# Two weight loads of a streamed MoE layer, cut so that the last 3 and 2 KB of each row travel in transfers of 69, 57 and 2 rows

## What is computed

```python
def expert_block(args):
    xb, e = args
    h = xb @ w_up[e] + b_up[e]
    h_glu = jnp.minimum(h[:, :D_FF], SWIGLU_LIMIT)
    h_lin = jnp.clip(h[:, D_FF:], -SWIGLU_LIMIT, SWIGLU_LIMIT)
    act = h_glu * jax.nn.sigmoid(SWIGLU_ALPHA * h_glu) * (h_lin + 1.0)
    return act @ w_down[e] + b_down[e]
```

## Time and profile before

| | us |
|---|---|
| median of 3 executions | 1082.04 |
| lowest and highest | 1081.49, 1084.55 |
| the profiled execution's own time | 1081.66 |
| its span, first to last instruction | 1079.8 |
| PE busy in the span | 1065.2 |

### The profile page before, as it was taken

One profiled execution on the slowest core, in us unless ns is written; L12 is line 12 of the kernel. 1 busy time (PEld: TensorE's weight loads), 2 busy tenths in 40 slices (PEclk: granted clock), 3 DMA queues, 4 the chain that ended last, 5 costly groups with the idle time before them and its releaser, 6 DMA issues.

```text
span 1079.8 us, 13215 instructions
## 1 busy us (share of the span) xinstructions
PE 1065.2 (99%) x5687; PEld 445.8 (41%) x5688; DVE 361.4 (33%) x572; ACT 152.8 (14%) x302; POOL 11.9 (1%) x28
## 2 busy tenths in 40 slices
PE   9999999999999999999999999999999999999997
PEld 7888664333333333333333333333333333333332
DVE  3376534233322233332222233323232232232234
ACT  2121144111111101111111110011111101101113
POOL 1000010000000000000000000000000000000002
PEclk9999999999999999999999999999999999999999
DMA  8875969999999999999999999999999999999995
GB/s 291 305 276 199 402 214 390 419 425 426 427 429 433 431 430 429 433 427 434 429 429 429 434 431 430 429 429 432 433 432 427 432 430 433 423 427 428 424 413 188
DMA packets 45515, 431.47 MB, mean 400 GB/s; under 512 B 4968, under 2 KB 20364, under 8 KB 25872
## 3 DMA queue, kind: packets, MB, share of 16 engines
q1 hardware_dynamic: 44848, 430.41, 95.3%
q10 hardware_dynamic: 608, 0.20, 0.1%
HBM read 427.00 MB, written 3.48 MB: 399 GB/s over the span
## 4 chain that ended last, share of the span: by engine, by line
PE 87%; DMA 11%; issue 0%; ACT 0%; DVE 0%; POOLq 0%; DVEq 0%; ACTq 0%; POOL 0%
PE bank L1035 39%; PE bank L1054 16%; DMA ring_all<-in_w_up 10%; PE bank L716 9%; PE bank L1102 6%; PE bank L1009 4%; PE bank L1046 2%; PE bank L826 2%; PE bank L1017 2%; PE bank L1027 1%; PE bank L1095 1%; PE bank L669 1%; PE bank L1114 1%; DMA ring_all<-in_w_in 1%; PE bank L834 1%; PE bank L1140 1%
## 5 line engine op out<-in xcount | busy, mean ns | idle before, releaser
L1035 PE MATMUL bank<-ring_all,work 128*64 128x512 f32 x2040 | 482.9, 600 | 4.9 <-DMA ring_all<-in_w_up 4.9
L1035 PEld LDWEIGHTS bank<-ring_all,work 128*64 128x64 f32 x2040 | 133.9, 136 | 253.4 <-issue 243.9
L1054 PE MATMUL bank<-ring_all,work 128*64 128x512 f32 x992 | 225.3, 596 | 0.0
L1887 DVE TENSOR_TENSOR h_tok<-h_tok,bank 128x1024 f32<-128x1024 f32 (+1 forms) x67 | 81.7, 1220 | 234.2 <-PE bank L1102 228.3
L1054 PEld LDWEIGHTS bank<-ring_all,work 128*64 128x64 f32 x992 | 68.4, 137 | 128.1 <-issue 128.0
L716 PE MATMUL bank<-work,ring_all 128*128 128x264 f32 x384 | 87.1, 387 | 0.5 <-DMA ring_all<-in_w_in 0.5
L716 PEld LDWEIGHTS bank<-work,ring_all 128*128 128x128 f32 x384 | 72.3, 190 | 13.1 <-DMA ring_all<-in_w_in 1.1
L1857 DVE TENSOR_TENSOR work<-bank,bias_up 128x1024 f32<-128x1024 f32 x32 | 39.2, 1224 | 113.9 <-PE bank L1046 113.9
L1102 PE MATMUL bank<-work 64*128 64x512 f32 (+1 forms) x268 | 75.1, 637 | 0.0
L1874 DVE TENSOR_TENSOR work<-work 128x512 f32<-128x512 f32 x32 | 22.2, 692 | 106.5 <-ACT work L1453 106.4
L1437 ACT ACTIVATE work<-bank 128x264 f32<-128x264 f32 x32 | 12.5, 391 | 313.1 <-PE bank L1027 313.1
(11 more groups left out here) (238 smaller groups left out, 550.6 us busy)
## 6 DMA issues: line engine op xcount, KB each, us to landing
ring_all<-in_w_up SPq DMA_DIRECT2D x40, 4096.0 KB, 33.5
ring_all<-in_w_down SPq DMA_DIRECT2D x20, 4096.0 KB, 34.5
ring_all<-in_w_up SPq DMA_DIRECT2D x33, 2048.0 KB, 15.2
ring_all<-in_w_down SPq DMA_DIRECT2D x15, 2048.0 KB, 18.4
ring_all<-in_w_up SPq DMA_DIRECT2D x29, 1024.0 KB, 10.4
ring_all<-in_w_down SPq DMA_DIRECT2D x18, 1024.0 KB, 11.9
ring_all<-in_w_in SPq DMA_DIRECT2D x13, 1024.0 KB, 5.0
ring_all<-in_w_out SPq DMA_DIRECT2D x4, 1024.0 KB, 11.6
```

What stands on the lines that cost most here:

```text
L1035: mm = pe.matmul(bank[half * CAP:(half + 1) * CAP, up_bank(n) + b, :].rearrange("q (k p) -> q p k", k=KT), x, src[half][:, b * 512:(b + 1) ...
L1054: mm = pe.matmul(bank[half * CAP:(half + 1) * CAP, Y, :], av[:, 2 * i + k, :], src[:, k * D + half * 512:k * D + (half + 1) * 512], start= ...
L1887: tt(rows, rows, bank[0:m, b:b + 2, :], ALU.add).then_inc(comb_added, 1)
```

## The change

Two pairs are treated apart: the one with chunks 2 and 3 of `w_up` of expert 16 (chunks 96 and 97 of the list) and the one with chunks 2 and 3 of expert 25 (chunks 150 and 151). Of their 32 KB rows only the first 29 KB and the first 30 KB are fetched by the transfer of 128 rows. The remaining 768 and 512 floats of each row (3 KB and 2 KB) come by three more transfers, of rows 0 to 68, 69 to 125, and 126 to 127, issued right behind it on the same queue. All four raise the same semaphore, and the count that PE waits for is raised by 3 x 16 to match. Nothing else changes.

```diff
+UNEVEN = {(16, 2): 768, (25, 2): 512}
+FEW_ENGINES = (slice(0, 69), slice(69, 126), slice(126, 128))
...
+        uneven = {place["u", e, j]: cols for (e, j), cols in UNEVEN.items()}
...
-            seen[s % RING] += 1
+            seen[s % RING] += 1 + (len(FEW_ENGINES) if s in uneven else 0)
             signal.append((s % RING, 16 * seen[s % RING]))
...
                     if s in pairs:
                         sp.wait_ge(mm_done, s - RING + 2)
-                        sp.dma_start(ring_all[:, s % RING:s % RING + 2, :].rearrange("p a n -> p (a n)"),
-                                     pair_src(stream[s])).then_inc(landed[s % RING], 16)
+                        pair = ring_all[:, s % RING:s % RING + 2, :].rearrange("p a n -> p (a n)")
+                        cut = 8 * FF - uneven.get(s, 0)
+                        sp.dma_start(pair[:, 0:cut], pair_src(stream[s])[:, 0:cut]).then_inc(landed[s % RING], 16)
+                        if s in uneven:
+                            for few in FEW_ENGINES:
+                                sp.dma_start(pair[few, cut:], pair_src(stream[s])[few, cut:]).then_inc(landed[s % RING], 16)
                         continue
```

## The result

| | before | after |
|---|---|---|
| median | 1081.51 us (6 runs) | 1089.27 us (6 runs) |
| lowest and highest | 1080.96, 1084.55 | 1087.64, 1091.40 |
| the profiled execution | 1081.66 | 1090.00 |
| its span | 1079.8 | 1088.1 |

The ratio is 1.0064, 95% interval 1.005 to 1.0078: slower by 5 to 8 us. The forecast was 1091.5.

What follows compares the result with a forecast made beforehand. The weight stream and PE were taken as limits side by side. Carriers +10.0 and +6.7 us, less a 6.5 us lead, gave 10.2, trimmed to +9.5: median 1091.5 us, range 1082 to 1096.5.

Steps and rivals of the forecast that it cites:

- the shared path: Main case at both changed pairs: engines writing into the same partitions share one path, slowing the new rows; +9.5 us, chance 0.58.
- Nothing is shared: Rival at the changed pairs: engines are the limit, not where they write; about +0.2 us, 1082.3, chance 0.20.
- spread over many engines: Rival: the new narrow transfers run on many engines, so nothing is uneven; 1082.2 us, chance 0.06.
- The engines that gain nothing: At the changed pairs, engines relieved of rows were to gain nothing, their own rows waiting beside the new ones.
- The carriers' rate: Three engines bringing the new rows (carriers) get 0.45 of full rate at both pairs: +16.7 us for a carrier.
- The two side figures of the sum: The total recomputed at other rates for the new rows: +8.2 us at 0.49, +12.3 us at 0.40.
- The lead: Earliest engines are 6.5 us ahead of the last at 916 us, bounds 5 to 8, absorbing that much lateness.
- the run-out: End of the stream: few engines late, most done early, shown by a share of 0.2 for 6 us or more.
- the carriers are not the early ones: Rival: engines bringing the new rows have no lead to spend; 1088.7 or 1098.7 us, chance 0.14.
- Where PE stands: PE's weight waits grow from 4.9 to about 14 us, first between 640 and 720 us, largest just behind 867.
- SP: Six more issues on SP, up to 0.45 us each, 2.7 us; covered by its waiting, so cost nothing.

Runs made afterwards that it cites:

- the two halves: Ten pairs' 3 KB tails (experts 9 to 18) by two transfers of 64 rows, against one of 128 rows: 1110.49 us, ratio 1.0271 to the kernel before.
- the two phases of three rows: Load-only kernel, three-row transfers of 16 KB behind whole pairs: 0.611 us a row into those engines' own partitions, 1.25 us into three others'.
- six carriers: Changed kernel with tails in transfers of 114, 12 and 2 rows, so six engines carry about half as much each: 1091.29 us, ratio 1.0086.
- the run with the second portion in two: Changed kernel with expert 25's 2 KB tails replaced by 1 KB each at experts 24 and 26: 1090.82 us, ratio 1.0077.

## Why the prediction was right

**Direction, mechanism and size.** +9.5 us was forecast and +7.8 measured between the medians, 5.4 to 8.4 by the ratio's interval; the shared path was the likeliest case, and it is what the runs show. The size owes something to luck, since two terms were wrong in opposite directions (below). "Nothing is shared" fell with the two halves (+28 us) and the two phases of three rows; "spread over many engines" with the share of 0.19.

**The engines that gain nothing.** This is the step that was wrong, though the sum hides it. The text said of the fourth engine that it "gains nothing, since its own rows wait beside it". It loses. The windows of the changed kernel move 330 instead of 436 GB/s from 595 to 610 and 379 instead of 432 from 860 to 880, which is 1.59 and 1.06 MB, at 431 GB/s 3.7 and 2.5 us of the whole stream, not of three engines. Its packet records say the same: 29 KB rows take 1.21 us on the mean where the single transfer of 128 rows has 1.11. Followed from row to row, an engine without new rows takes from 587.8 to 609.8 us for eight rows of 29 KB and eight of 32 KB, 22.0 us, which at 1.10 and 1.215 us a row are 18.5. The pair issued at 867.7 before and at 870.6 after is the same one. Its signals from the engines of the late group came in by 906.2 before and by 910.5 after, 4.2 us later, although each of them had 1.5 us fewer to do. It stays hidden in the sum, because in the changed kernel the carriers end behind them.

**The carriers' rate.** Taken as 0.45 of the full rate, measured 0.200 and 0.135 us a row against 0.121 and 0.085, that is 0.61 and 0.63. The term is 43 x 0.200 - 0.9 = 7.7 and 43 x 0.135 - 0.6 = 5.2, 12.9 us instead of 16.7. It was too large by 3.8. What was missing is that the carriers' own whole rows are slowed as well: in the pair behind each changed one they take 1.24 to 1.37 us instead of 1.215, which is 0.2 to 1.2 us for eight rows. The last signals of that pair come at 914.8 instead of 906.2, +8.6 us, in the profiled executions, whose times differ by 8.3. The two side figures of the sum don't come out of it: with the same 0.7 taken off, the working at a rate of 0.49 gives +8.0 and not +8.2, and a rate of 0.40 gives +11.8 and not +12.3.

**The lead.** 6.5 us was an estimate from the run-out. By the signals of that same pair before, seven engines were through within 2.6 us of the first, and the other nine between 5.0 and 6.7. After the change three come at 9.5, 10.5 and 11.4 us behind the first, four are left within 1.4, and a fifth comes at 3.2. A signal doesn't name its engine, but the packet records of the first changed pair, followed from row to row, show that the carriers were early ones: they began their 3 KB rows at 596.7, 598.1 and 598.1 us, while the last of the other engines was through with its 29 KB rows at 604.0. So "the carriers are not the early ones" fell. At the second pair they were early no longer (their part of it ended at 867.2, 868.4 and 869.8, that of the others between 861.7 and 868.8): the lead is spent once, as the sum had it. With six carriers, the three added ones had less lead.

Where the lead comes from was not asked in the prediction, and the packets suggest an answer. Between 150 and 1066 us the kernel before has 39 packets of 16 KB on a queue of the kind "instruction". An engine that takes one needs mostly 11.26 us for eight rows instead of 9.72. Those 39 times 1.5 us over nine engines are 6.5 us, about the distance of the late group. Most of those that could be followed fell on late engines. No run tried it.

**Where PE stands.** Forecast: waits of about 14 us, measured 11.3. The first was expected between 640 and 720 and ended at 626.9, a little early; the largest just behind 867, and it was 5.05 us, ending at 876.3. PE hardly noticed the first pair, as said, with no wait at 609; its last signal came at 607.6 instead of 603.4, 4.2 us later where 5 was forecast. The run-out was to show a share of 0.2 for 6 us or more. It shows 0.60, 0.18 and 0.06 in windows of 2 us from 1068 to 1074, so about 4 us of it.

```profile
1068.00:1070.00 2.00, 2.00 (x14) 0.74 (x12) 1.22 (x1) 0.00 (x0) 0.00 (x0) 1.00 0.60 230
1070.00:1072.00 2.00, 2.00 (x15) 0.59 (x13) 1.22 (x1) 0.00 (x0) 0.00 (x0) 1.00 0.18 71
1072.00:1074.00 2.00, 2.00 (x20) 1.18 (x20) 1.21 (x1) 0.38 (x1) 0.00 (x0) 1.00 0.06 25
```

In the earlier trace rows the share fell through 0.70, 0.59 and 0.36: there a large group was late, here few engines are.

**SP.** Costed at nothing, and rightly: the three more issues at each place took 0.99 us, and its next issue came 8 us later.

**What stays open.** Why the meeting of two engines costs more than the sharing of one rate. In the ten pairs by halves, 8 tail rows at 0.07 us too much and 8 long rows at 0.075 too much are 1.1 us of the 2.8 that a pair lost. The whole rows of 32 KB between 380 and 720 us, 2867 of them at 0.066 us too much, are another 1.2 us a pair on each of 16 engines. So 2.3 us are found in slower rows; why the meeting slows the rows behind as well was not taken apart.

## What to carry to other kernels

Levelling a stream by handing rows to engines that are ahead did not work in any of the forms tried here, since the rows still go to the partitions of the others: both sides slow down, and at the first changed pair the engines that were to be relieved of 0.9 us lost 3.5 instead. Judge a stream by GB/s next to the share, since the share stayed at 0.96 and more while engines got in each other's way. And a delay put where PE had 15 us to spare cost as much as one put where it had 0.85 us, since here the stream sets the end.

## What was not expected of the hardware

- Two transfers of 64 rows in place of one of 128, with the same bytes on every engine, cost 2.8 us a pair of 4 MB for tails of 384 KB a pair; one transfer of 128 rows for the same tails cost nothing that could be measured (ratio 1.0001).
- Whole rows of 32 KB took 1.213 us beside transfers in the carriers' own partitions and up to 2.51 us beside the same transfers 12 partitions further on.
- The granted clock fell to 0.51 behind a wait of 5.05 us of PE, and somewhat (0.90 over 10 us) behind one of 2.12 us at 907.9 in the run with the second portion in two; it stayed at 1.00 behind one of 2.75 us at 874.9 in the run with six carriers. The length of the wait alone doesn't decide it. The run with the cuts at experts 9 and 10 lost as much at a clock of 1.00 throughout.
